# PEER expert slots of one token tile issued among the other tiles' front work, in one unrolled list of items

## The reference

```python
def layer(x, cond, lw, rope, ctx_cache):
    sh1, sc1, g1, sh2, sc2, g2 = jnp.split(jax.nn.silu(cond) @ lw['w_mod'] + lw['b_mod'], 6, axis=-1)
    h = rmsnorm(x, lw['g_attn_norm']) * (1 + sc1) + sh1
    mix, new_ctx = branches(h, lw, rope, ctx_cache)      # attention A, gMLP B, windowed attention C
    x = x + g1 * mix
    h = rmsnorm(x, lw['g_ffn_norm']) * (1 + sc2) + sh2
    x = x + g2 * peer(h, lw['w_pq'], lw['peer_keys'], lw['peer_u'], lw['peer_v'])
    return x, new_ctx

def one(hb):                                             # peer, for one tile of 128 tokens
    q = (hb @ w_pq).reshape(t, P_HEADS, 2, P_QDIM // 2)
    sc = jnp.einsum('thpd,hpkd->thpk', q, keys)
    ...                                                  # top 16 of each half, top 16 of the 256 sums
    act = jax.nn.gelu(jnp.einsum('thkd,td->thk', u_tab[eidx], hb))
    return jnp.einsum('thk,thkd->td', gate * act, v_tab[eidx])
```

## Time and profile before

| | |
|---|---|
| median of 3 runs | 5882.09 us (5868.98 to 5891.37) |
| the profiled execution, first to last instruction | 5888.0 us |
| PE busy | 4851.9 us, 82% |
| DVE busy | 3117.5 us, 53% |
| POOL busy | 1547.3 us, 26% |
| ACT busy | 1068.8 us, 18% |
| DMA | 1509.10 MB, 256 GB/s over the span |

### The profile page before, as it was taken

One profiled execution on the slowest core, in us unless ns is written; L12 is line 12 of the kernel. 1 busy time (PEld: TensorE's weight loads), 2 busy tenths in 40 slices (PEclk: granted clock), 3 DMA queues, 4 the chain that ended last, 5 costly groups with the idle time before them and its releaser, 6 DMA issues.

```text
span 5888.0 us, 54180 instructions
## 1 busy us (share of the span) xinstructions
PE 4851.9 (82%) x13846; PEld 2304.7 (39%) x13846; DVE 3117.5 (53%) x7277; ACT 1068.8 (18%) x2738; POOL 1547.3 (26%) x1465
## 2 busy tenths in 40 slices
PE   9999999967777777777799999999777777777776
PEld 3578544522222222222235784445222222222222
DVE  2454112176676677676625541122666676676775
ACT  0223100122111211211102220011221121211211
POOL 0200000034334334443302000000333443434443
PEclk9989999999999999999999999999999999999999
DMA  6110111199999999999861002112999999999998
GB/s 260 49 37 1 75 50 72 67 382 372 379 372 368 387 377 386 393 374 381 346 247 57 20 1 75 65 65 100 383 371 388 359 378 379 379 377 387 376 378 338
DMA packets 213890, 1509.10 MB, mean 256 GB/s; under 512 B 24652, under 2 KB 26316, under 8 KB 33996
## 3 DMA queue, kind: packets, MB, share of 16 engines
q0 software_dynamic: 185040, 1344.88, 58.0%
q1 hardware_dynamic: 20880, 141.57, 6.2%
q10 hardware_dynamic: 7800, 20.57, 1.0%
HBM read 1503.65 MB, written 3.28 MB: 256 GB/s over the span
## 4 chain that ended last, share of the span: by engine, by line
PE 44%; DMA 22%; DVE 20%; issue 7%; DVEq 3%; POOL 2%; ACT 1%; ACTq 0%; POOLq 0%
DMA arena<-in_experts,arena 21%; PE ps L473 12%; DVE sq L1299 11%; PE ps L697 7%; PE ps L664 4%; PE ps L645 3%; PE ps L594 3%; PE ps L622 2%; PE ps L656 2%; POOL arena L442 2%; PE ps L493 2%; DVE arena L1202 2%; PE ps L606 2%; DVE arena L1205 1%; DVE arena L1203 1%
## 5 line engine op out<-in xcount | busy, mean ns | idle before, releaser
L697 PE MATMUL ps<-arena 128*128 128x512 f32 x5120 | 2539.0, 645 | 972.0 <-ACT arena L888 934.3
L1299 DVE CUSTOM_DVE_ANT_0 sq<-arena,z 128x1024 f32<-128x1024 f32 x1280 | 1569.8, 1226 | 1024.3 <-DMA arena<-in_experts,arena 957.8
L442 POOL DMA_INDIRECT arena<-in_experts,arena x1280 | 1418.6, 1108 | 2408.2 <-PE ps L697 1980.5
L697 PEld LDWEIGHTS ps<-arena 128*128 128x128 f32 x5120 | 995.3, 203 | 2514.8 <-ACT arena L888 1398.3
L473 PE MATMUL ps<-arena 128*128 128x512 f32 (+3 forms) x1920 | 757.8, 551 | 0.0
L881 ACT ACTIVATE arena<-arena 128x2 f32<-128x2 f32 x640 | 130.1, 204 | 2704.3 <-DVE arena L1299 2704.3
L426 POOL TENSOR_SCALAR ss<-ss 128x1 f32<-128x1 f32 (+3 forms) x86 | 29.7, 345 | 1846.7 <-DVE ss L961 1328.5
L473 PEld LDWEIGHTS ps<-arena 128*128 128x128 f32 x1920 | 364.2, 191 | 370.4 <-issue 336.7
L888 ACT ACTIVATE arena<-ident,arena 128x128 f32<-128x128 f32 x1280 | 439.5, 393 | 128.3 <-DVE arena L1309 127.7
L664 PE MATMUL ps<-arena 128*128 128x128 f32 (+1 forms) x992 | 268.2, 429 | 2.5 <-ACTq L745 2.5
L1119 DVE TENSOR_REDUCE negm<-ps 128x1 f32<-128x768 f32 (+4 forms) x160 | 118.9, 744 | 264.7 <-PE ps L601 164.0
(11 more groups left out here) (166 smaller groups left out, 3447.3 us busy)
## 6 DMA issues: line engine op xcount, KB each, us to landing
arena<-in_weights SPq DMA_DIRECT2D x122, 1024.0 KB, 6.8
arena<-in_experts,arena POOLq DMA_INDIRECT x1280
big<-mod_rows ACTq DMA_DIRECT2D x16, 512.0 KB, 8.6
arena<-in_weights SPq DMA_DIRECT2D x8, 576.0 KB, 4.5
arena<-in_weights SPq DMA_DIRECT2D x4, 768.0 KB, 4.7
arena<-in_weights SPq DMA_DIRECT2D x6, 512.0 KB, 4.2
big<-in_g_norm ACTq DMA_DIRECT2D x4, 512.0 KB, 12.4
x<-in_x_sample POOLq DMA_DIRECT2D x4, 512.0 KB, 5.9
```

The source lines that it names most:

```text
L442: pool.indirect_dma_start(out=ring[s % RING], out_offset=None, in_=ins["experts"], in_offset=bass.IndirectOffsetOnAxis(ap=ihead[:, s:s + 1 ...
L697: last = MM(a[:, c * 512:(c + 1) * 512], diag[s % RING], ring[s % RING][:, D + c * 512:D + (c + 1) * 512], start=False, stop=False)
L1299: last = V.tensor_tensor_reduce(out=sq[:], in0=ring[r][:, 0:D], in1=h2[:, i, :], scale=1.0, scalar=0.0, op0=ALU.mult, op1=ALU.add, accum_o ...
```

## The change

The loop over layers is gone. One list of items, `ITEMS`, made by `schedule()`, is walked by every engine, and each engine emits its part of an item or nothing.

- The items of a front are spread out, and *groups* of two expert slots of another tile stand among them. `Spread.stretch(front, groups)` puts the groups at equal distances of a cost of TensorE time that a table gives (`tensor_cost`). A group is `E` (two dots, then four small operations on ACT), with `Ewt` (weights and diagonals) one group later and `Emm` (the matmuls) two groups later.
- In order: the prompt's front alone; the samples' front with merging and routing of tiles 1 and 2, holding the 64 groups of tile 0; merging and routing of tiles 3 and 4, holding those of tile 1; the choice for tiles 3 and 4, the next layer's `mod` and the prompt's next front, holding the 192 groups of tiles 2, 3 and 4. Layer 1 does the same, but its last 192 groups have only the choice of tiles 3 and 4 (8 items `tk2`) beside them.
- Since the prompt and the two pairs of sample tiles are merged and routed apart, the weights of `gate`, `proj`, `out` and `pq` are loaded three times in a layer, those of the input projections twice. The blocks loaded come to 290 MB in all. The ring has NU = 3 buffers.
- A slot is fetched by two gathers of 4 KB rows, u and v. u has 4 buffers (3 for the prompt's slots) and v has 5 (4 for the prompt's). `gather_u` waits for the dot that used the buffer, `gather_v` for the matmuls that used it; on POOL's queue the v of slot n-2 follows the u of slot n.
- 1/sqrt is made on DVE by `root`: a bit shift for a first guess and three Newton steps, 12 operations for one column, 15 for several, each behind a drain.
- The copy of the transposed exponentials goes from DVE to ACT. Scores and transposes now have two pairs of PSUM banks.
- gelu of the dots is made with Square, Copy and two Tanh (`E` on ACT); sigmoid in merging is made with Tanh. The choice works on whole tiles: `tk1` (top 16 of the scores of one q), `tk2` (a quarter of a tile's pairs), `tkg`.

```diff
-NU = 5
-NB1, NB2 = 2, 3
-RING = 8
+NU = 3
...
+GROUPS = {0: (0,), 1: (1, 2), 2: (3, 4)}
...
+    def group(self):
+        self.items.append(("E", self.dotted))
+        self.dotted += 1
+        if self.dotted - self.weighted > 1:
+            self.weigh()
+        if self.weighted - self.added > 1:
+            self.add()
...
+    def stretch(self, front, groups):
+        total = sum(tensor_cost(i) for i in front)
+        at = put = 0
+        for i in front:
+            while put < groups and at * groups >= (put + 0.5) * total:
+                self.group()
+                put += 1
+            self.items.append(i)
+            at += tensor_cost(i)
+        while put < groups:
+            self.group()
+            put += 1
...
+def prompt_front(l, mods):
+    before = norm_and_inputs(l, PROMPT) + [("outlat", l)] + attention(l, PROMPT)
+    return interleave(before, mods) + merge_and_route(l, 0, GROUPS[0], True) + choose(l, 0)
+def sample_first(l):
+    return [("ctxA", l)] + norm_and_inputs(l, SAMPLE) + attention(l, SAMPLE) + merge_and_route(l, 1, GROUPS[1], True) + choose(l, 1)
+def schedule():
+    s = Spread()
+    m = mod_items(0)
+    s.items += [("start",), ("consts", 0)] + m[:8] + prompt_front(0, m[8:]) + [("g2", 0, 0)]
+    s.stretch(sample_first(0), NGRP)
+    s.stretch(merge_and_route(0, 2, GROUPS[2], False) + choose(0, 2), NGRP)
+    s.stretch(choose(0, 3) + choose(0, 4) + [("consts", 1)] + mod_items(1) + prompt_front(1, []), 3 * NGRP)
+    s.flush()
+    s.stretch(sample_first(1), NGRP)
+    s.stretch(merge_and_route(1, 2, GROUPS[2], False) + choose(1, 2), NGRP)
+    s.stretch(choose(1, 3), NGRP)
+    s.stretch(choose(1, 4), NGRP)
+    s.stretch([], NGRP)
+    s.flush()
+    return s.items
...
+UBUF = [(s % SLOTS) % (3 if ETILES[s // SLOTS][1] == 0 else 4) for s in range(NSLOT)]
+UBUF = [7 if b == 3 else b for b in UBUF]
+VBUF = [(s % SLOTS) % (4 if ETILES[s // SLOTS][1] == 0 else 5) for s in range(NSLOT)]
+VBUF = [8 if b == 4 else 3 + b for b in VBUF]
+LEAD = 2
...
+            def gather_u(n):
+                l, t = ETILES[n // SLOTS]
+                if n % SLOTS % 32 == 0:
+                    pool.wait_ge(*ready("tk2", l, t, n % SLOTS // 32))
+                if SAME_U[n] is not None:
+                    pool.wait_ge(dot_done, SAME_U[n] + 1)
+                if UBUF[n] == EXT_U and t == 1 and n % SLOTS < 4:
+                    pool.wait_ge(*full("pq", l, 1, 15))
+                gather(n, index_u, UBUF[n])
+            def gather_v(n):
+                l, t = ETILES[n // SLOTS]
+                if SAME_V[n] is not None:
+                    pool.wait_ge(slot_used, SAME_V[n] + 1)
+                if VBUF[n] == EXT_V and t == 1 and n % SLOTS < 5:
+                    pool.wait_ge(*full("mT", l, 1))
+                gather(n, index_v, VBUF[n])
+            v = 0
+            for n in range(NSLOT):
+                if n % SLOTS == 0 and ETILES[n // SLOTS][1] < 2:
+                    while v < n:
+                        gather_v(v)
+                        v += 1
+                gather_u(n)
+                while v <= n - LEAD:
+                    gather_v(v)
+                    v += 1
+            while v < NSLOT:
+                gather_v(v)
+                v += 1
...
-                    with pool.Fori(0, TURNS) as t:
-                        for s in range(BODY):
-                            if s % HALF == 0:
-                                pool.wait_ge(half_ready.sem, l * half_ready.layer + t * 2 + (2 * i * TURNS + s // HALF + 1))
-                            pool.wait_ge(slot_used.sem, l * slot_used.layer + t * BODY + (i * SLOTS + s + 1))
-                            alone(pool)
-                            pool.indirect_dma_start(
-                                out=ring[s % RING], out_offset=None, in_=ins["experts"],
-                                in_offset=bass.IndirectOffsetOnAxis(ap=ihead[:, s:s + 1], axis=0)
-                            ).then_inc(g_land[s % RING].sem, 16)
...
-                    nc.gpsimd.tensor_scalar(ss[:, at:at + cols], ss[:, at:at + cols], 1.0 / width, EPS,
-                                            ALU.mult, ALU.add).then_inc(mid_ready.sem, 1)
-                    pool.wait_ge(mid_ready.sem, mid_ready.at(l, e + 1))
-                    alone(pool)
-                    nc.gpsimd.tensor_tensor(rstd[:, at:at + cols], ss[:, at:at + cols],
-                                            mhalf[:].to_broadcast([P, cols]), ALU.pow).then_inc(rstd_ready.sem, 1)
...
+            def root(n, width):
+                a, y, t = ss[:, 0:n], rs[:, 0:n], rt[:, 0:n]
+                TS(a, a, 1.0 / width, EPS, ALU.mult, ALU.add)
+                dve.drain()
+                TS(t.bitcast(U32), a.bitcast(U32), 1, None, ALU.logical_shift_right)
+                dve.drain()
+                TS(y.bitcast(U32), t.bitcast(U32), -1.0, 1597463007.0, ALU.mult, ALU.add)
+                dve.drain()
+                for _ in range(3):
+                    if n == 1:
+                        STT(t, y, rs[:, 0:1], a, ALU.mult, ALU.mult)
+                    else:
+                        TT(t, y, y, ALU.mult)
+                        dve.drain()
+                        TT(t, t, a, ALU.mult)
+                    dve.drain()
+                    TS(t, t, -0.5, 1.5, ALU.mult, ALU.add)
+                    dve.drain()
+                    TT(y, y, t, ALU.mult)
+                    dve.drain()
...
+                elif kind == "E":
+                    n0 = GRP * item[1]
+                    c = n0 % 8
+                    for n in range(n0, n0 + GRP):
+                        dve.wait_ge(row_land[UBUF[n]], 16 * TURN_U[n])
+                        V.tensor_tensor_reduce(out=sq[:], in0=ring[UBUF[n]], in1=h2_of_slot(n), scale=1.0, scalar=0.0,
+                                               op0=ALU.mult, op1=ALU.add, accum_out=dots[:, n % 8:n % 8 + 1]).then_inc(dot_done, 1)
+                        dve.drain()
+                    s = n0 % SLOTS
+                    TT(dgate[:, c:c + GRP], dots[:, c:c + GRP], gate[ETILES[n0 // SLOTS][1]][:, s:s + GRP], ALU.mult)
+                    dve.drain()
+                elif kind == "Ewt":
+                    c = GRP * item[1] % 8
+                    dve.wait_ge(tanh_done, item[1] + 1)
+                    STT(wts[:, c:c + GRP], dth[:, c:c + GRP], 1.0, dgate[:, c:c + GRP], ALU.add, ALU.mult).then_inc(wts_done, 1)
...
+                elif kind == "Emm":
+                    for n in (GRP * item[1], GRP * item[1] + 1):
+                        s = n % SLOTS
+                        if s == 0 and n:
+                            pe.wait_ge(acc_free, n // SLOTS)
+                        elif s == 0:
+                            pe.wait_ge(*ready("mod", 0, 11))
+                        pe.wait_ge(row_land[VBUF[n]], 16 * TURN_V[n])
+                        pe.wait_ge(diag_done, n + 1)
+                        for c in range(2):
+                            last = MM(acc[:, c * 512:(c + 1) * 512], diag[n % 4], ring[VBUF[n]][:, c * 512:(c + 1) * 512], start=s == 0, stop=s == SLOTS - 1)
+                        last.then_inc(slot_used, 1)
```

2053 lines of the change are left out of this document (1038 added, 1015 removed).

## The result

The changed kernel takes 6242.78 us in the median of 4 runs (6237.27 to 6257.44), the kernel before 5884.93 us in the runs beside it. The ratio is 1.061, 95% interval [1.059, 1.064]: slower by 358 us, of which the prediction foresaw 168. The time lies in the stated range and on the side forecast, but the size is over twice the one forecast. The profiled execution spans 6245.7 us.

The account below looks back on a forecast made before the run. Fronts were taken as PE-bound, experts as DMA-bound. Stages summed as 430 + 2 x 1058 + 2 x 443 + 1440 + 1168 + 10 = 6050 us; main case 5912 to 6200, stated range 5730 to 6400.

Parts of the forecast that it names:

- opening: Layer 0's `mod` and the prompt's front alone, without groups: 109 + 213 + 110 more for one tile alone, taken as 430 us.
- fourth stage: 192 groups among choices, the next `mod` and the prompt's front, merge and route: together 1440 us.
- last stage with tail: The last 198 groups at 5.9 us, POOL the bound, 1168 us; then a tail of 10 us.
- The failed step: Layer 1's last part: 8 choice pieces of 12 us taken as filled by what the rings hold, so no cost.
- The fallback in the text: Choice pieces in layer 1's last part: if the rings cover none, 8 x 6 = 50 us more.
- POOL's pace: Groups standing alone: four gathers, 40 to 45% caught in dots, 5.9 us a group, above DMA's 5.42.
- The norm stage: Samples' norms with groups: DVE becomes the bound at 307 us against PE's 254; taken as 330 us.
- The sign that was named: Samples' norm stage: DVE busiest of all and PE under 0.8, waiting for DVE's roots.
- Attention: Samples' attention with groups: units 3.74 us apart for 3.34, 26 us a layer; stage taken as 345 us.
- The allowance of 260 us: Middle stages: 182 + 78 us added to the larger engines' times for engines waiting on each other in order.
- Short rings: Rival: v's 5 buffers turn too slowly, 7 us a group, 6400 us in all; chance 0.17 (6200 to 6500).
- cheap coupling: Rival: slack and rings even out the engines' loads, so the change gains, 5700 us; chance 0.27 (5550 to 5850).

Follow-up runs that it names:

- quarters: Changed kernel with each `tk2` cut into four items and layer 0's choices of tiles 3 and 4 dealt out among the `mod` items: 6142.41 us.
- the three lengths above: Choice pieces of 12.7 us (whole, 6242.78 us), some 6.5 us (halves, 6214.21 us) and some 3 us (quarters, 6142.41 us), costing 8, 3 and 0.7 us each.
- last run: Changed kernel with split gathers into a ring of 8 in the last stage, and h2 in PSUM and 2 KB rows in the last 64 groups: 6237.05 us.

## Why the prediction was wrong in size

Stage by stage, forecast and measured (from first and last dots and items): opening 430 and 438; samples' fronts 1058 twice, and 1043 and 1045; pair two 443 twice, and 459 and 442; fourth stage 1440 and 1514; last stage with tail 1178 and 1305. Sum 6050 and 6246. Of the 196 us missed, 127 are in the last stage and 74 in the fourth; the other five terms come to -5 together.

- **The failed step** is the choice: the pieces in the last stage "are taken as filled by what the rings hold", and the choice of tile 2 in its first groups got no price beyond theirs. Measured, the first 8 groups took 102 us where 8 x 5.9 = 47 would stand (55 us), and the 128 groups 6.36 for 5.9 us (59 us); in the fourth stage the two stretches of choices took 275 and 144 for 255 and 105 (59 us). Together 173 of the 196. The causes differ. In the 8 groups DVE is full, and its work there was left out of the sum. In the 128 the pieces stop the gathers: one stood DMA still for 7 us, no choice gave 65 us back, and quarters 44 us in these groups with the same work (100 in all). For the 59 us of the fourth stage only this much is tried: quarters dealt out among `mod` took 32 us off groups 128 to 224. The fallback in the text, "if none is covered they cost 8 x 6 = 50 us more", was near for the eight pieces, but it was made a side case: a piece of 12 us was held against two groups of DMA, some 11 us, where by the three lengths above only 2.5 to 4.5 us of a piece cost nothing.
- **POOL's pace, 5.9 us a group: right number, by luck.** The 64 groups without choice took 5.83. The argument was that gathers caught in dots put POOL above DMA's 5.42. As many were caught as forecast (42% lasted over 0.96 us, for 40 to 45%), but each waited 0.34 us and not 0.6: 1.08 us in the mean, so 5.5 us a group for the 5.9. And with none caught a group still took 5.78 or 5.73 us. What the halved gathers cost against joined ones is 0.47 us a group in the same ring; neither caught gathers, nor bytes, nor ring length, nor all three explain it (5.66 us with all gone), and the cause stays open. The Trainium skill, SBUF — State Buffer, § Who interferes with whom, says that a DVE instruction with two SBUF inputs contends with a GpSimd instruction that reads SBUF. The trace agrees: gathers fell from 1072 to 941 ns with one SBUF input. It is not what set the time. The Trainium skill, DMA: Bandwidth & Descriptors, § Bandwidth, asks for DMAs of 1 MiB or more. The trace agrees in the direction: gathers of 1 MiB (8 KB rows) moved 379 to 397 GB/s and those of half the size 344 to 366. The forecast used 5.42 us of DMA for both sizes.
- **The norm stage.** Its time was right (319 for 330 us) and so was its bound, DVE: 236 us busy and 50 of short gaps (307 with 55 of drains forecast), for PE's 264. The sign that was named, DVE busiest and PE under 0.8, failed (0.74 and 0.83), since busy shares leave the gaps out. Without the Newton steps the stage is 46 us shorter. The text's 4/5 of 230 for PE is 184, not 189.
- **Attention.** 343 us for 345. The 0.4 us put on a unit for two pairs of banks was small: by the starts of their row maxima units stand 3.76 us apart in the kernel before and 4.40 in the list without overlap, where the copy on ACT and the lower clock count as well. With groups between them PE is at 0.93.
- **Coupling.** The allowance of 260 us for stages in order fits: these stages came out within 16 us each. Which single waits make it up was not tried. (The larger engines of the opening are 109 + 213 = 322 in the text, but 340 in its sum of larger engines; the forecast does not hang on it.)
- **Rivals.** Short rings: not the cause in the last stage, where a ring of 8 with split gathers changed nothing; elsewhere it was not tried. That the change gains by cheap coupling: overlap did bring 971 us, but what it was bought with costs 1331: one-tile and pair-wise fronts with weights loaded more often, roots and choices outside the groups (1102 us), and split gathers and short prompt rings (229 us).

## What to carry to other kernels

Before two streams are merged into one order, price the merged version without any overlap: here it was 1331 us above the kernel before, and that is what the overlap has to pay back first. In a common order the length of an item counts beside the amount: hold each item against the time that the rings of the other stream really cover (here 2.5 to 4.5 us, not the 11 of two groups), and cut it if it is longer. Cutting does not help where the engine itself is full; count its short gaps as well as its busy time to see that. And when a transfer is halved to save memory, measure its rate and its issue cost at the new size first; one such edit cost the old kernel 395 us alone.

## What the runs showed of the hardware that was not expected

- Indirect gathers of 128 rows moved 379 to 397 GB/s with rows of 8 KB (kernel before, joined gathers) and 344 to 366 GB/s with rows of 4 KB (kernel before with split gathers, last stage of the changed one), at busy shares of 0.93 to 0.98. With rows of 2 KB the share was 0.63 to 0.64 at 178 to 185 GB/s: half the bytes take two thirds of the DMA engines' time.
- A gather on POOL that nothing held lasted 0.94 us, and the pause to the next was 0.30 us at the least, with rows of 2, 4 and 8 KB alike (last run, changed kernel, kernel before).
- A gather on POOL lasted 941 ns beside dots that have one of their two inputs in PSUM, and 1072 ns in the mean (up to 1.9 us) beside the same dots with both in SBUF; the dot took 1.22 us either way.
- With split gathers POOL now and then waited for a queue that the profile doesn't name: 24 times, up to 3.4 us, in the kernel before with split gathers, never in it without; up to 3.7 us in the last run above.
